# The last 128 tokens of a decoder block: down projection in narrower column groups, final norm on two engines

## The reference, cut to what matters

```
h   = gelu(conv(x1 @ w_ffn_gate)) * (x1 @ w_ffn_up)      # 2048 x 2816
y   = ALPHA * x1 + h @ w_ffn_down                        # 2048 x 1024
mu, var = mean and variance of each row of y
out = (y - mu) * rsqrt(var + 1e-5) * ln2_g + ln2_b
```

## Time and profile before

| | |
|---|---|
| median of three runs | 985.53 us (985.52 to 985.93) |
| the profiled execution | 986.06 us, span of its slowest core 984.5 us |
| spans of the eight cores | 977.9 to 984.5 us |
| PE busy | 935.1 us, 95% of the span |
| VectorE, ScalarE, GpSimd busy | 59%, 46%, 27% |
| last matmul of core 1 | ends at 975.98 us |
| last VectorE instruction | ends at 982.08 us |

### The profile page before, as it was taken

One profiled execution on the slowest core, in us unless ns is written; L12 is line 12 of the kernel. 1 busy time (PEld: TensorE's weight loads), 2 busy tenths in 40 slices (PEclk: granted clock), 3 DMA queues, 4 the chain that ended last, 5 costly groups with the idle time before them and its releaser, 6 DMA issues.

```text
span 984.5 us, 17162 instructions; the slowest of 8 cores (977.9 to 984.5 us)
## 1 busy us (share of the span) xinstructions
PE 935.1 (95%) x4992; PEld 473.3 (48%) x4992; DVE 583.4 (59%) x1066; ACT 454.6 (46%) x832; POOL 264.2 (27%) x303
## 2 busy tenths in 40 slices
PE   4779999899999999999999999999999999999996
PEld 1335555466666664444444444444444444444442
DVE  4456875565433333565468778763777666665755
ACT  0226577667777772245545565652003555553000
POOL 4364455532312125355413323240000000000000
PEclk9789999999999999999999999999999999999998
DMA  8944310162332229953265664589333644440221
GB/s 116 179 102 82 69 39 13 24 109 34 62 61 55 34 33 192 191 164 98 108 119 135 149 135 91 105 206 176 109 107 109 127 68 84 69 82 1 100 94 64
DMA packets 42460, 95.76 MB, mean 97 GB/s; under 512 B 6592, under 2 KB 15296, under 8 KB 41728
## 3 DMA queue, kind: packets, MB, share of 16 engines
q0 software_dynamic: 22432, 52.37, 33.2%
q1 hardware_dynamic: 19936, 42.29, 13.2%
HBM read 125.89 MB, written 16.78 MB: 145 GB/s over the span
## 4 chain that ended last, share of the span: by engine, by line
PE 84%; DMA 7%; DVE 3%; issue 3%; POOL 1%; SPq 1%; ACT 1%; DVEq 0%; POOLq 0%; ACTq 0%
PE ps L420 83%; DMA wga<-wg 2%; DMA ropeS<-ropeS 2%; SPq L417 1%; DMA xT<-xT 1%; DMA k<-hst 1%; DVE t L440 1%; PE ps L424 1%; POOL P L440 1%; DVE hT L440 1%; POOL hst L440 1%; DVE row L453 0%; DMA k<-oh 0%; DVE cbuf L453 0%; DVE PT L815 0%
## 5 line engine op out<-in xcount | busy, mean ns | idle before, releaser
L420 PE MATMUL ps<-x1T,wgu 128*128 128x512 bf16 x1408 | 310.9, 379 | 3.9 <-DVE hT L440 2.1
L420 PEld LDWEIGHTS ps<-x1T,wgu 128*128 128x128 bf16 x1408 | 137.1, 98 | 171.0 <-issue 7.9
L453 DVE SCALAR_TENSOR_TENSOR cbuf<-abuf,small,cbuf 128x512 f32<-128x512 f32 x176 | 145.5, 827 | 99.6 <-ACT cbuf L437 89.9
L437 ACT ACTIVATE PT<-ps 128x512 bf16<-128x512 f32 (+1 forms) x288 | 154.2, 572 | 89.7 <-PE ps L420 83.1
L420 PE MATMUL ps<-wd,hT 128*128 128x512 bf16 x704 | 152.3, 379 | 0.0
L420 PE MATMUL ps<-PT,Vp 128*128 128x256 bf16 (+1 forms) x584 | 105.9, 264 | 5.8 <-DVE PT L815 5.5
L420 PE MATMUL ps<-q,k 72*128 72x256 bf16 x576 | 107.5, 268 | 2.4 <-DMA k<-oh 2.4
L420 PEld LDWEIGHTS ps<-wd,hT 128*128 128x128 bf16 x704 | 68.9, 98 | 83.0
L437 ACT ACTIVATE abuf<-ps 128x512 f32<-128x512 f32 x88 | 52.4, 595 | 110.1 <-PE ps L420 110.1
L411 POOL DMA_DIRECT2D wgu<-wgu x44 | 23.9, 543 | 289.3 <-PE ps L420 282.7
L420 PE MATMUL ps<-xT,wqk 128*128 128x512 bf16 x256 | 67.7, 408 | 20.0 <-DMA xT<-xT 19.8
(11 more groups left out here) (104 smaller groups left out, 1059.3 us busy)
## 6 DMA issues: line engine op xcount, KB each, us to landing
wgu<-wgu POOLq DMA_DIRECT2D x44, 512.0 KB, 5.5
xres<-x SPq DMA_DIRECT2D x16, 512.0 KB, 5.2
x1s<-row SPq DMA_DIRECT2D x16, 512.0 KB, 2.8
row<-x1s SPq DMA_DIRECT2D x16, 512.0 KB, 9.6
out<-row SPq DMA_DIRECT2D x32, 256.0 KB, 2.0
wd<-wd POOLq DMA_DIRECT2D x22, 256.0 KB, 11.4
wga<-wg POOLq DMA_DIRECT2D x16, 256.0 KB, 5.1
wgp<-wg POOLq DMA_DIRECT2D x16, 256.0 KB, 5.8
```

Source lines behind the costliest of these rows:

```text
L420: S.op("pe", lambda e: e.matmul(out, lhsT, rhs, start=start, stop=stop), reads=[lhsT, rhs], writes=[out])
L437: S.op("act", lambda e: e.activation(out=out, in_=in_, func=func, **kw), reads=rd, writes=[out])
L453: S.op(eng, lambda e: e.scalar_tensor_tensor(out=out, in0=in0, scalar=scalar, in1=in1, op0=op0, op1=op1), reads=rd, writes=[out])
```

## The change

For the last tile of the second half `p8` calls a new function, `last_tile`. The first 512 columns are multiplied as before, but their statistics are taken in two pieces of 256. The other 512 are multiplied in two groups of 256 columns, each in a bank of its own (one more bank), with its own add and statistics. The aggregate takes four pieces of statistics, held in a new small tile `sfin` at the place of `identb`, which is no longer in use. The first pass over columns 0 to 511 is recorded ahead of the reciprocal. Then GpSimd normalises columns 768 to 1023 in three operations, `tensor_scalar` (subtract the mean, times the reciprocal root), times `ln2g`, plus `ln2b`, and VectorE does columns 0 to 511 and 512 to 767. Two writes go out as before, the second of which now waits for both engines.

```
+    sfin = T("sfin", [128, 4, 6], F32, 0)
...
+    def bns(out, in_):
+        S.op("dve", lambda e: e.bn_stats(out=out, in_=in_), reads=[in_], writes=[out])
+
+    def out_dma(t_, rw, a, b, key):
+        S.dma("sp", lambda e: e.dma_start(out=out_d[t_ * 128:(t_ + 1) * 128, a:b], in_=rw[:, a:b]),
+              reads=[rw[:, a:b]], writes=[key])
+
+    def last_tile(t_, rw, mv, bks, dmm):
+        for f in range(NF):
+            dmm(7, bks[0], 0, f)
+        stt("dve", rw[:, 0:512], rw[:, 0:512], ALPHA, bks[0][:, :], ALU.mult, ALU.add)
+        bns(sfin[:, 0, :], rw[:, 0:256])
+        bns(sfin[:, 1, :], rw[:, 256:512])
+        for i, bk in ((2, bks[1]), (3, nbank())):
+            a, b = i * 256, (i + 1) * 256
+            for f in range(NF):
+                mm(bk[:, 0:256], hT[:, f, 896:1024], wd[f][:, a:b], f == 0, f == NF - 1)
+            stt("dve", rw[:, a:b], rw[:, a:b], ALPHA, bk[:, 0:256], ALU.mult, ALU.add)
+            bns(sfin[:, i, :], rw[:, a:b])
+        S.op("dve", lambda e: e.bn_aggr(out=mv[:, 0:2], in_=sfin[:].rearrange("p a b -> p (a b)")),
+             reads=[sfin[:]], writes=[mv[:, 0:2]])
+        ts("dve", mv[:, 1:2], mv[:, 1:2], EPS, None, ALU.add)
+        act(mv[:, 2:3], mv[:, 1:2], AF.Sqrt)
+        stt("dve", rw[:, 0:512], rw[:, 0:512], mv[:, 0:1], ln2g[:, 0:512], ALU.subtract, ALU.mult)
+        recip(mv[:, 2:3], mv[:, 2:3])
+        ts("pool", rw[:, 768:1024], rw[:, 768:1024], mv[:, 0:1], mv[:, 2:3], ALU.subtract, ALU.mult)
+        tt("pool", rw[:, 768:1024], rw[:, 768:1024], ln2g[:, 768:1024], ALU.mult)
+        tt("pool", rw[:, 768:1024], rw[:, 768:1024], ln2b[:, 768:1024], ALU.add)
+        stt("dve", rw[:, 0:512], rw[:, 0:512], mv[:, 2:3], ln2b[:, 0:512], ALU.mult, ALU.add)
+        out_dma(t_, rw, 0, 512, ("out", t_, 0))
+        stt("dve", rw[:, 512:768], rw[:, 512:768], mv[:, 0:1], ln2g[:, 512:768], ALU.subtract, ALU.mult)
+        stt("dve", rw[:, 512:768], rw[:, 512:768], mv[:, 2:3], ln2b[:, 512:768], ALU.mult, ALU.add)
+        out_dma(t_, rw, 512, 1024, ("out", t_, 1))
...
+            if half == 1 and tl == 7:
+                last_tile(t_, rw, mv, bks, dmm)
+                continue
```

## The result

The changed kernel takes 989.57 us (median of 6 runs, 987.97 to 991.3); the kernel before, over 6 runs, 985.75 us (985.52 to 986.2). The ratio is 1.0042, 95% interval 1.0032 to 1.0053: slower by 0.42%, some 4 us, outside the predicted range. The profiled execution was the quickest of the six, 987.97 us, so spans are of little use for a difference of this size. The end of the program, counted from the start of its last matmul, is the same on the eight cores of a profile to a few hundredths of a us in both kernels, and is what I compare.

A forecast was written before the change was run, and what follows sets the result against it. The prediction took the tail behind the last matmul as what the change can touch: arithmetic 0.76 us shorter, 0.67 with the matmuls' 0.09 cost, so 985.53 - 0.67 = 984.86 us, told as 984.9; range 984.0 to 986.3.

The forecast's parts named there:

- issue and landing of the last write: After the last arithmetic: same 256 KB write, landing 2.0 us in the median, taken to move with the arithmetic's end and cancel.
- The rival with a load of 6 us: Load before GpSimd's first tensor_scalar: 986.1 us at 1.28 us, 990.9 at the skill's some 6 us; chance 0.04.
- The matmuls: Second half's last tile: 44 matmuls of 256 columns at 0.110 us replace 22 of 512, costing 0.09 us on the path.
- The statistics and the pause: Only the last quarter's add and statistics, 0.43 us each, stay on the path; VectorE's 0.36 us pause falls into idle time.
- GpSimd's tensor_scalar: First GpSimd operation on columns 768 to 1023: taken at 0.60 us, bounded by 0.24 and 1.26.
- The rival of a dear tensor_scalar: GpSimd's tensor_scalar costs up to 2.49 us, time 986.8 us, gain zero at 1.27; chance 0.10.
- The estimate from the Trainium skill, GPSIMD Engine Reference, section Engine selection: GpSimd's one-input tensor_scalar streams 256 columns in 0.21 us, making the sum 0.2 to 0.3 us better.
- The two tensor_tensor: GpSimd's last two operations on columns 768 to 1023, 256 columns each: 0.71 us apiece.
- Turns: VectorE's two-SBUF-input passes and GpSimd's operations alternate in the tail; GpSimd ends at +5.34, gain 0.67 us; chance 0.60.
- The sum of the arithmetic: Tail after the last matmul's end: GpSimd ends the arithmetic at +5.34 us against +6.10, 0.76 us less.

## Why the prediction was wrong, point by point

- **What closes the program.** The step that failed is the sentence that issue and landing of the last write move "with the end of the arithmetic and cancels". They nearly do (SyncE starts its DRAIN 2.21 us behind the arithmetic before, 2.28 after), but they are not all that ends this program: the engines also wait for GpSimd's DRAIN. The tail grew by 4.07 us, while SyncE was ready only 0.20 us later (+8.71 to +8.91); the other 3.9 us are the wait for the DRAIN. The row was in the trace of before (8.2 us at 879.8, line 228), hidden by 96 us of matmuls. The prediction read the end of VectorE, ScalarE and SyncE and not that of the engine that the change brings in.
- **The rival with a load of 6 us** had about the right size (990.9 us) for the wrong reason: nothing comes before the first tensor_scalar (it starts 0.20 us behind the reciprocal and costs 1.22 us alone, first or second); the 6.1 us come behind the last operation. The rival's price was that of the Trainium skill, GPSIMD Engine Reference, section Instruction dispatch: some 6 us for the first call of a freshly loaded routine. No run here shows it before an operation.
- **The matmuls** cost what was forecast: 0.109 us each against 0.110 assumed. From the start of the last 512-column matmul, the last one ends after 5.18 us, where it was 5.13: 0.05 us, forecast 0.09.
- **The statistics and the pause.** The aggregate started 0.10 us behind its statistics, took 0.26 where 0.22 was assumed, and the pause of 0.36 was off the path, as forecast. The place of the pause, the 2236th entry of VectorE in the trace with its waits counted, is the aggregate before and the wait for the last quarter after. (The forecast's 1152 entries between two pauses are not the shortest distance: before the change there is one at the reciprocal of 921.91 too, 128 entries ahead of the last.) The reciprocal followed the first pass by 0.66 us (forecast 0.67) and ended 2.41 us behind the last matmul's end; forecast 2.38.
- **GpSimd's tensor_scalar** was mis-sized: 1.22 us alone against 0.60, which was taken as "just under the two-input operation of the same width"; it is nearly what two inputs of 512 columns take, 1.26. The rival of a dear tensor_scalar had this part right. The estimate from the Trainium skill, GPSIMD Engine Reference, section Engine selection (one-input operations near line rate; by its clock an estimate of 0.21 us of streaming), was further off. The two tensor_tensor were 0.72 each; forecast 0.71.
- **Turns.** The tensor_scalar waited for the 512-column pass, as the earlier trace rows had it. But it did not hold the two passes behind. The forecast had them stretched to 0.6 us or more; they kept 0.49 and 0.48. The earlier trace rows show tensor_tensor only, and that was carried over to a one-input operation without a row for it. GpSimd's own tensor_tensor operations met no pass of VectorE here (978.49 against 977.99), so nothing is learnt on them. What the 0.24 us are by which the short passes delayed the tensor_scalar stays open.
- **The sum of the arithmetic.** Forecast: end 5.34 us after the last matmul's end; measured 6.35, before 6.10. Even without the DRAIN the change would have lost some 0.3 us. The whole error of 1.0 us lies up to the end of the tensor_scalar, 4.62 us after the last matmul's end where 3.62 was forecast: 0.62 its own price, 0.24 the two short passes, the rest small. From there to the end forecast (1.72) and measured (1.73) agree by luck: the forecast has GpSimd wait for VectorE twice, and in the trace it waits only for its own results.

## What to carry to other kernels

Each engine's list ends in a DRAIN, and on GpSimd it ended 6.1 us behind the last operation here, for each of the three kinds tried (tensor_tensor, memset, a chain of three). Work on GpSimd is free near the end only if it is over well before: by an estimate from these tails, by 2.6 us behind the start of the last matmul (8.93 less 6.35), which is 3.9 us ahead of the end of VectorE's last pass. When a change brings an idle engine into the tail, read what that engine does after its last row, by the instructions of the line that ends the block, and ask when the other engines meet it. And the gain that was hoped for was to be had without it: a pass moved into the wait for ScalarE and narrower last groups took 1.3 us off the end by the tails, about 1 us by the timed runs (ratio 0.9990), on VectorE alone.

## What the runs showed of the hardware that was not expected

- GpSimd's DRAIN ended 6.11 to 6.13 us behind its last arithmetic operation in seven kernels, for a memset of 0.10 us as for a chain of three operations; behind the issue of a weight load it was 7.7 us in the kernel before. The DRAIN at the head of the program took 0.17 to 0.19 us.
- A one-input tensor_scalar with two scalars from memory, 128 x 256 fp32, takes 1.22 us on GpSimd, more than the two-input tensor_tensor of the same size (0.72).
- VectorE's 256-column passes with two SBUF inputs took 0.49 and 0.48 us inside the 2.00 us of a tensor_scalar of GpSimd; 0.49 is also the estimate for such a pass alone (0.75 for 512 columns, 0.26 less for 256 fewer). A GpSimd row includes the time that the operation is held, but the second pass (977.51 to 977.99) lies in its last 0.83 us, and its own time is 1.22. Under a tensor_tensor a 512-column pass took 1.44 for 0.7. The Trainium skill, SBUF — State Buffer, section SBUF: two separate sides, describes the shared ports as a lock that one instruction keeps to its end, with the other blocked. The tensor_tensor rows agree, this one does not, and the measurement decides.
- Matmuls of 128 columns, each with its own weight load of 128 rows, followed each other at 0.056 us. With groups of 384 and 128 the last matmul starts 4.96 us behind the last 512-column one, against 4.75 before, and by its own shorter time ends 0.05 us later: the narrow groups cost next to nothing on PE.
